# One block for projections and attention, with nine convolution taps moved from ScalarE and DMA to VectorE

## What is computed

```python
proj = h @ w_in                       # q (8 heads of 64), k, v (2 heads), and the two halves of a GLU
kv_ctx = hc @ w_in[:, k and v columns]
q, k = rope(rms_norm(q)), rope(rms_norm(k));  k_ctx = rms_norm(k_ctx)
attn = softmax([sink, q k_ctx, q k within +-128 tokens]) @ [v_ctx, v]
u = depthwise_conv(ga * sigmoid(gb), 31 taps) + conv_b     # 512 channels
u = silu(layer_norm(u))
x = x + g1 * (concat(attn, u) @ w_out)
x = x + g2 * (gated MLP of modulate(rms_norm(x)))          # w_up, width-3 conv, w_down
```

## Time and profile before

| | us |
|---|---|
| median of 3 runs | 1359.11 (1356.21 to 1361.14) |
| the profiled execution | 1354.87 |
| its span in the profile | 1353.0 |
| GLU products | about 60 to 154 |
| projections to q, k, v and the last transposes | about 155 to 255 |
| attention | about 258 to 492 |
| output projection, MLP | the rest, from about 507 |

### The profile page before, as it was taken

The page is one execution under the profiler, slowest core; times in us unless marked ns, Lnnn a source line. Parts: engine busy times, 40 slices in busy tenths (PEclk is TensorE's granted clock), DMA queues, the critical chain, the costliest instruction groups (busy, mean ns, idle before and its releaser), DMA issues. The chain is left out here.

```text
span 1353.0 us, 15984 instructions
## 1 busy us (share of the span) xinstructions
PE 1244.5 (92%) x6181; PEld 1031.7 (76%) x6181; DVE 677.9 (50%) x979; ACT 453.2 (33%) x723; POOL 137.5 (10%) x148
## 2 busy tenths in 40 slices
PE   5899899689869869999999999999999969999997
PEld 1378788589857857877888888888888858887886
DVE  1589955578634544434344444434344444447445
ACT  4542356556535653553222222222222211110110
POOL 2100111254551020000000000000000000004001
PEclk9899989688879979999999999999999989999999
DMA  9222545599994005213111111111111041113112
GB/s 377 66 85 76 121 93 110 125 206 264 256 260 120 1 0 202 79 47 93 47 47 47 47 55 53 47 47 47 47 47 47 16 155 47 47 47 109 47 47 78
DMA packets 86772, 126.77 MB, mean 94 GB/s; under 512 B 6842, under 2 KB 60210, under 8 KB 85700
## 3 DMA queue, kind: packets, MB, share of 16 engines
q1 hardware_dynamic: 75796, 87.65, 19.4%
q0 software_dynamic: 9776, 34.28, 12.8%
q10 hardware_dynamic: 1152, 4.19, 0.8%
HBM read 85.74 MB, written 8.39 MB: 70 GB/s over the span
## 5 line engine op out<-in xcount | busy, mean ns | idle before, releaser
L1331 PE MATMUL ps<-hx,uph 128*128 128x512 f32 x672 | 261.4, 389 | 0.0
L1332 PE MATMUL ps<-hx,uph 128*128 128x512 f32 x672 | 261.4, 389 | 0.0
L1335 PE MATMUL ps<-hx,upl 128*128 128x512 f32 x672 | 206.9, 389 | 0.0
L1133 DVE TENSOR_TENSOR upl<-up_raw,uph 128x1024 fp32r<-128x1024 f32 x44 | 53.8, 1226 | 263.9 <-ACT uph L1130 263.9
L1130 ACT ACTIVATE uph<-up_raw 128x1024 fp32r<-128x1024 f32 x44 | 46.5, 1060 | 339.5 <-PE ps L1335 328.6
L1464 PE MATMUL ps<-dnh,ah 128*128 128x512 f32 x352 | 138.1, 392 | 13.2 <-DVE al L1515 13.2
L1332 PEld LDWEIGHTS ps<-hx,uph 128*128 128x128 f32 x672 | 126.2, 188 | 26.2
L1331 PEld LDWEIGHTS ps<-hx,uph 128*128 128x128 f32 x672 | 126.2, 188 | 26.1
L1335 PEld LDWEIGHTS ps<-hx,upl 128*128 128x128 f32 x672 | 126.2, 188 | 26.1
L1465 PE MATMUL ps<-dnl,ah 128*128 128x512 f32 x352 | 137.5, 391 | 0.0
L1466 PE MATMUL ps<-dnh,al 128*128 128x512 f32 x352 | 137.5, 391 | 0.0
(11 more groups left out here) (235 smaller groups left out, 2159.7 us busy)
## 6 DMA issues: line engine op xcount, KB each, us to landing
up_raw<-in_w_up SPq DMA_DIRECT2D x44, 512.0 KB, 3.8
wm<-in_w_mod SPq DMA_DIRECT2D x32, 512.0 KB, 7.6
sums<-wm POOLq DMA_DIRECT2D x32, 512.0 KB, 8.6
dn_raw<-in_w_down SPq DMA_DIRECT2D x44, 256.0 KB, 2.7
wm<-in_w_mod SPq DMA_DIRECT2D x8, 1024.0 KB, 20.6
conv_y<-u POOLq DMA_DIRECT2D x14, 512.0 KB, 4.5
cacc<-cacc POOLq DMA_DIRECT2D x11, 512.0 KB, 4.5
xs<-in_x ACTq DMA_DIRECT2D x8, 512.0 KB, 14.3
```

The costliest lines, as they stand in the source:

```text
L1133: dve.tensor_tensor(out=upl[:, g], in0=up_raw[:, g], in1=f(uph[:, g]), op=ALU.subtract).then_inc(up_lo, 1)
L1331: pe.matmul(o, uph[:, g, k, :], hx[:, k, 0, c_], start=(k == 0), stop=False)
L1332: pe.matmul(o, uph[:, g, k, :], hx[:, k, 1, c_], start=False, stop=False)
L1335: last = pe.matmul(o, upl[:, g, k, :], hx[:, k, 0, c_], start=False, stop=(k == KT - 1))
```

## The change

1. Blocks s1 and s3 become one: no meeting of the engines between them. Semaphores and buffers are laid out anew; each wait that the block's end had covered is now written out (`drained`, `qkT_out`, `v_out`).
2. The first transposed item comes in tile 3, not in tile 2. Tile m uses the pair of banks of `(m + 2) % 3`.
3. Group 0's scores are issued in tile 8 (behind k = 5 and 6) and tile 9 (behind k = 1 and 2). Its maxima stand on VectorE behind tile 7's low parts (heads 0, 1) and behind tile 8's rotations (heads 2, 3). Its `exps` stand on ScalarE ahead of the reading of tile 8 and of tile 9. Its scores use banks 0 and 1 alone.
4. Tile 8's items follow the loop over tiles; what remains of tile 9 (sums, roots, high and low parts) goes into group 0, its items into group 1 (j = 0 to 2).
5. The summed tile gets 22 products, all in the projections. The other nine taps are VectorE instructions of 1024 columns (`join_taps`), one a group in groups 2 to 6 and two each in groups 7 and 8, behind the join of the two sums in group 1. Products 16 to 21 with an even number go through another buffer.
6. The 153 steps of the other tiles: six instead of twelve behind the last GLU product, 33 instead of 16 in tiles 2 to 7, five a group in groups 1 to 8, none in group 0.
7. GpSimd begins the modulation vectors when the last item has been placed (group 1); SyncE loads their first tiles behind tile 9's matmuls.

```diff
-        TAP_QKV = (0, 0) + (2,) * TT
-        TAP_GRP = 6
+        TAP_GLU = (0, 11, 11, 13, 13, 13, 13, 6)
+        TAP_QKV = (0, 0, 7, 6, 6, 3, 6, 5, 0, 0)
+        TAP_GRP = 5
+        MOVE = 16
-        P_BLOCK = 24
+        P_BLOCK = 22
...
+            return u[:, 0, 0:T] if i % 2 else cacc[:, DVE_TILES[2], :] if i < MOVE else u[:, DVE_TILES[1], 0:T]
...
+            if i == MOVE:
+                act.wait_ge(tap_done, 2 * NCS)
...
+        def join_taps(dve, n):
+            if n == 0:
+                for r in range(2):
+                    dve.wait_ge(sum_in[r], 16 * (P_BLOCK // 2 - 1))
+                ins = dve.tensor_tensor(out=SUM[0], in0=SUM[0], in1=SUM[1], op=ALU.add)
+            else:
+                i = P_BLOCK + n - 1
+                dve.wait_ge(join_done, n)
+                v = SUM[0].rearrange("p (two s) -> p two s", two=2)
+                ins = dve.scalar_tensor_tensor(out=v, in0=by_parity(u_plain[:, i:i + T]), scalar=cols[:, C_CONVW + i * CTL + AT:C_CONVW + i * CTL + AT + 1],
+                                               in1=v, op0=ALU.mult, op1=ALU.add)
+            ins.then_inc(join_done, 1)
+
+        JOINS = TAPS - P_BLOCK + 1
+        JOIN_AT = ((), (3,), (3,), (3,), (3,), (3,), (3,), (1, 3), (1, 3))
...
+            FIRST_SCORES = {(NK - 2, 5): 0, (NK - 2, 6): 1, (NK - 1, 1): 2, (NK - 1, 2): 3}
...
+                sp.wait_ge(qkv_mm, NK)
...
+                pool.wait_ge(qkT_out, len(items))
...
+                def drained(m):
+                    pe.wait_ge(v_out, m + 1)
+                    pe.wait_ge(k_mul, m + 1)
+                    if m >= CT:
+                        pe.wait_ge(q_mul, m - CT + 1)
...
+                    if it == 0:
+                        pe.wait_ge(v_out, NK)
+                        pe.wait_ge(q_mul, TT)
...
-                        if m >= 2 and k in (2, 4, 6) and turned < items_upto[m - 1]:
-                            turn(turned)
+                        if m >= 3 and k in (2, 4, 6) and turned < items_upto[m - 1]:
+                            turn_qk(turned)
                             turned += 1
+                        if (m, k) in FIRST_SCORES:
+                            scores(0, FIRST_SCORES[m, k])
...
+                        if n == 1 and j < 3:
+                            turn_qk(turned)
+                            turned += 1
...
+                    if m >= NK - 2:
+                        for hl in range(2 * (m - NK + 2), 2 * (m - NK + 2) + 2):
+                            exps(0, hl)
+                    read_tile(m)
+                    if m == NK - 1:
+                        break
+                    product(act)
+                    roots(m)
+                    k_high(m)
                     if m >= CT:
+                        q_high(m)
                         product(act)
...
+                        if n == 0 and j == 0:
+                            q_high(NK - 1)
+                        if n == 0 and j == 1:
+                            roots(NK - 1)
+                        if n == 0 and j == 2:
+                            k_high(NK - 1)
+                        if n == 1 and j < 3:
+                            place(placed)
+                            placed += 1
...
-                    elif n == LN - 1:
-                        for r in range(2):
-                            dve.wait_ge(sum_in[r], 16 * len(range(2 + r, TAPS, 2)))
-                        dve.tensor_tensor(out=cacc[:, AT, :], in0=cacc[:, AT, :], in1=conv_y[:], op=ALU.add).then_inc(tap_done, 1)
...
-                            if n < LN:
-                                taps(dve, TAP_GRP if n == LN - 1 and j == 3 else TAP_GRP // 4 + (j < TAP_GRP % 4))
+                            if n == 0 and j == 0:
+                                square_sums(NK - 1)
+                                rope_sums(NK - 1)
+                            elif n == 0 and j == 1:
+                                k_scaled(NK - 1)
+                            elif n == 0 and j == 3:
+                                low_halves(NK - 1)
+                            elif 0 < n < LN:
+                                taps(dve, TAP_GRP // 4 + (j < TAP_GRP % 4))
+                                if j in JOIN_AT[n]:
+                                    join_taps(dve, joined)
+                                    joined += 1
```

More of the change, by code:

```diff
@@ new lines, in values @@
+                def values(n, j):
+                    i, g, kts = head_steps(n)
+                    it = first_item[n] + j
+                    if j == 0 and n:
+                        pe.wait_ge(on_done, n)
+                    if j == 0 and n == 0:
+                        pe.wait_ge(qkT_out, items_upto[NK - 1])
+                    pe.wait_ge(pt_out, it + 1)
+                    for hl in range(GQ):
+                        last = pe.matmul(ps[:, 6, hl * HD:(hl + 1) * HD], pt[:, it % NPT, hl * P:(hl + 1) * P], vraw[:, kts[j], g, :],
+                                         start=(j == 0 and hl == 0), stop=(j == len(kts) - 1), skip_group_check=True)
+                    last.then_inc(pv_mm, 1)
@@ new lines, in turn_outputs, with mean_of @@
+                def turn_outputs(n):
+                    pe.wait_ge(on_done, n + 1)
+                    if n == 0:
+                        pe.wait_ge(qkT_out, len(items))
+                    bank_read(n + 1)
+                    for r in range(2):
+                        last = pe.transpose(ps[:, 7, r * P:(r + 1) * P], on[:, r * P:(r + 1) * P], ident[:])
+                    last.then_inc(oT, 1)
+                def mean_of(buf, hh, signal):
+                    for ct in range(CTL):
+                        last = pe.matmul(ps[:, 7, :], meanw[:], buf(ct)[:, half(hh)], start=(ct == 0), stop=(ct == CTL - 1))
+                    last.then_inc(signal, 1)
@@ L583, in place, with read_tile @@
                     act.activation(dst, src, ACT.Copy).then_inc(qkT_out, 1)
[L585 to L592 removed]
+                def read_tile(m):
+                    b, h0 = slot(m), (0 if m >= CT else NH)
                     act.wait_ge(qkv_mm, m + 1)
@@ new lines, in _ @@
+                placed = 0
+                act.wait_ge(const_done, 7)
+                for m in range(NK):
+                    while m >= 3 and placed < items_upto[m - 1]:
+                        place(placed)
[4 more added lines that the diff above has]
+                    read_tile(m)
+                    if m == NK - 1:
+                        break
+                    product(act)
+                    roots(m)
+                    k_high(m)
@@ L617, in _ @@
+                output_high(NGRP - 1)
+                for i in range(4):
+                    act.wait_ge(row_mm, 4)
+                    act.activation((g1b, g2b)[i // 2][:, half(i % 2)], ps[:, i, :], ACT.Copy).then_inc(row_out, 1)
             @block.vector
```

602 lines of the change are left out of this document (299 added, 303 removed).

## The result

| | before | after |
|---|---|---|
| median | 1360.12 (1356.21 to 1361.59, 4 runs) | 1315.54 (1313.02 to 1318.48, 4 runs) |
| the profiled execution | 1354.87 | 1318.48 |
| its span | 1353.0 | 1316.7 |

The ratio is 0.9677 with a 95% interval of 0.9643 to 0.9712: 44.6 us faster by the medians. The forecast was 1319, 40.0 less than before.

A forecast was written before the change was run, and what follows sets the result against it. TensorE, 92% busy, was taken as the bound, with gains from its idle and 1.2 GHz time. 9.0 - 1.2 + 8.4 + 22.1 + 1.7 = 40.0 off 1354.87 gives 1314.9; the median 4.2 higher, so 1319, range 1312 to 1326.

The forecast's parts named there:

- the seam: Tile 8's end to group 0's outputs: 31.5 us instead of 39.9, saving 8.4 before 1.2 for tile 8's scores.
- groups 1 to 8: Attention, group 0's to group 8's outputs: late products and adds go, 97.8 us against 119.9, saving 22.1.
- first transposes in tile 3: Projections, tile 2: TensorE's 5.83 us hole and 3 us of half clock go; gain taken as 9.0 us.
- scores in tile 8: Two heads' scores, about 0.6 us each, put tile 8's end 1.2 us later.
- group 2: Attention: takes over the burst in which GpSimd's first four multiplies slow VectorE; 14.0 us.
- groups 7 and 8: Attention: VectorE's five steps and two taps make 12.1 us; taken as 12.2 each, 24.4 together.
- behind group 9: Rest of the kernel after group 9: nothing touched, no change counted.
- a seam bound by ScalarE: Rival, chance 0.12: third items wait 4 us more, clock stays down into group 1; seam gives 0, time 1328.
- the moved taps meet GpSimd: Rival, chance 0.20: GpSimd's multiplies lengthen VectorE's taps; groups 1 to 8 save 12.2 instead of 22.1, time 1329.
- The waits were not all small: Rival, chance 0.08: groups at 10.9 us and no stall at third items; 8 us more gained, 1311.
- group 8's wait is gone: Opposing rival, chance 0.05: last adds or late VectorE keep group 8's wait, putting 15 us back; time 1334.
- nothing kept TensorE at 1.2 GHz: Opposing rival (slower), chance 0.03: seam and short waits hold TensorE at 1.2 GHz through group 8; time 1373.

The follow-up runs named there:

- experiment 1: The kernel before with only the first transposed item moved from tile 2 to tile 3; 1352.18 us, ratio 0.9945 against before.
- experiment 10: experiment 5 with all of tile 9's sums, roots, parts and items ahead of group 0's scores; 1320.91 us, ratio 0.9712 against before.
- experiment 5: The changed kernel with group 0's scores, maxima and Exp behind the loop over tiles; 1316.24 us, ratio 0.9667 against before.
- experiment 2: The kernel before without the last seven products of the summed tile and their adds; 1336.41 us, ratio 0.9857 against before.
- experiment 4: The changed kernel without GpSimd's 32 multiplies of w_mod with c, loads and adds kept; 1312.2 us, ratio 0.9637 against before.
- experiment 6: The changed kernel with eight VectorE steps moved from groups 1 to 8: five behind tile 8's low parts, three in group 0; 1313.86 us, ratio 0.9662.
- experiment 3: The changed kernel without the nine moved taps on VectorE, left out of the sum; 1312.11 us, ratio 0.9662 against before.
- experiment 11: The changed kernel with first scores behind the loop, tile 9's roots ahead of group 0's Exp, and VectorE's steps, join and taps spread anew; 1308.62 us, ratio 0.963.

## Why the prediction was right, by its steps

The time was inside the range, 3.5 below the forecast, and the direction and the main causes were as stated. That the sum comes so near is in part luck: the seam saved 2.3 us more than forecast and groups 1 to 8 saved 1.7 less, and the terms were read from an execution of before that was short at the seam and behind group 14, by some 3 us in each place if experiment 1's is the measure. By terms, between the profiled executions:

| step | forecast | measured |
|---|---|---|
| first transposes in tile 3 | 9.0 | 9.8, of which 0.8 ahead of tile 0 (7.6 when made alone, by medians) |
| scores in tile 8 | -1.2 | -1.1 (9.8 less 8.7) |
| tile 8's end to group 0's outputs | 31.5, saving 8.4 | 29.2, saving 10.7 |
| group 1 | 13.0 | 13.8 |
| group 2 | 14.0 | 11.7 |
| groups 3 to 6 | 46.4 | 47.7 |
| groups 7 and 8 | 24.4 | 26.35 |
| group 9 | saving 1.7 | saving 1.6 |
| modulation vectors' last add issued | near 405, price 0 | 394.01, price 0 |
| behind group 9 | untouched, 0 | 5.0 lost, of which 3.5 also in experiment 1 |

**First transposes.** The reasoning holds: no idle time at the item, in after and in experiment 1.

**The seam.** The chain of copies was right to half a microsecond: tile 9's matmuls end at t = 12.7 (13.1 forecast), the waits at the third items are 1.73 and 3.12 us (2.3 and 2.8). What came out better was group 0 behind them, 16.5 us from tile 9's end instead of 18.4. Its first turn begins at t = 17.5 (forecast 18.7), and from there it takes 11.7 us to the outputs (forecast 12.8). In that last part ScalarE is busy for 9.5 us, where the forecast, adding up durations of instructions that in the rows above overlap by about 0.1 us each, had 10.3; the 2.2 us left are near the 2.5 that it had for waits. The load at 229.91 cost nothing: it ends 2.07 us before the sums that its roots need, and the forecast counted nothing for it. The prediction treated the scores in the tiles, the single block and tile 9's remainder as one term, and that hid what the experiments showed: the first is worth under 1 us, the second by itself 0 to 3, the third about 7.5 us at group 0's outputs (263.66 in experiment 10, 256.14 in experiment 5) and 4.7 by the medians. The rival of a seam bound by ScalarE was wrong in its total (it gave 0, and 10.7 were measured) and right about the mechanism, for that part of the change alone.

**Groups 1 to 8.** The largest term, and its cause stands: without the late products (experiment 2) the kernel before has groups of 11.6 us at a clock of 1.00, and the wait of 13.18 us in group 8 is gone in every kernel without them. The size was off by 1.7 us in all, from two errors that partly cancel. Group 2 was put at 14.0 for a burst of four multiplies; it took 11.7. Groups 7 and 8 were put at 12.2 each, by adding up VectorE's work without the multiplies; with two taps and multiplies on each they took 13.2 and 13.1. Groups 3 to 6 are 11.9 instead of 11.6; without the multiplies (experiment 4) groups 3 to 6 took 10.8 each and groups 7 and 8 12.0 and 12.4. The prediction put the wait in group 8 down to full DMA engines; it left out that the last add stands 23.5 us in GpSimd's list first.

**The rival that the moved taps meet GpSimd** was right that the multiplies stretch groups 2 to 8, and wrong about which instructions pay. Taps stayed at 1.27 us but for one of 2.96; the 512-column steps took most of the loss. Its price, 9.9 us, was too high: without any multiply g0 to g8 is 7.7 us shorter, and part of that loss was in the forecast already, since before's groups had it too. The Trainium skill's section named there, taken strictly, would have one instruction wait for the whole of the other; the rows of group 5 show both kinds, a step of 0.74 grown to 1.39 under a multiply, and a tap of 1.28 that kept its time while the multiply that began inside it (314.70) took 1.89 us, longer than the 1.11 and 1.43 of others. The tap of 351.28 does not fit the strict reading: it began 0.45 us before the multiply of 351.73, and yet it was the tap that grew, to 2.96, while the multiply kept 1.43. There the measurement decides.

**The other rivals** fell. The waits were not all small (11.9 us a group, not 10.9); group 8's wait is gone; nothing kept TensorE at 1.2 GHz from group to group: group 1 had a mean clock of 0.81, groups 2 to 6 of 1.00.

**The tail** was the one thing left out. The forecast held everything behind group 9 fixed, and there the profiled execution of after lost 5.0 us at a lower clock. For 3.5 of them the reason lies in before's execution, as experiment 1 shows. The rest stands in group 14, which took 12.7 us in the traces of before and of experiment 1, and 13.8 or more in the other twelve; why is open. Experiments 4 and 6 lost time in group 9 at a lower clock, and experiments 3 and 11 did not. What decides whether such a stretch falls to 1.2 GHz stays open.

## What to carry to other kernels

Look first at work whose result comes by a late transfer: without the late adds and their products g0 to g8 fell by 27 us, the largest single effect here. Ask of such an add both how long it takes under load and how long it stands in its engine's list before it is issued. When scores or any other work of the next stage are pulled forward into a full stage, look at the queue of the engine that must serve both (here ScalarE's Exp beside Sqrt); moving the remainder of the old stage back, beside the new stage, was worth about 7.5 us at that place and 4.7 by the medians, and pulling the new one forward less than 1. When work is moved to an engine that looks half idle, place it where that engine waits (behind the loop and in groups 0 and 1 here), at a single piece per group, and away from a neighbour that slows it; the kernel of experiment 11, which goes by this, is the only one whose times lie clear of the changed kernel's. And before a loss or gain is read from two traces, see where each lies among its kernel's times: one that is 5 us below its median lends its luck to every comparison.

## What the runs showed of the hardware that was not expected

- **Multiplies of GpSimd make a group longer even when VectorE has time left.** With 48.8 us of VectorE's work in five groups (experiment 3) they took 57.8 us, and with 48.5 (experiment 2) 58.2; with 48.4 us and no multiplies (experiment 4), 53.6.
- **A local gain is not always a gain at the end.** Experiments 3, 4 and 6 were 6.5, 7.7 and 6.0 us shorter than after between group 0's and group 8's outputs. At the end the same executions were 8.7, 2.7 and 3.5 us shorter than after's (1318.48), and 3.4, 3.3 and 1.7 by the medians: experiment 3 kept its gain, 4 and 6 lost a good part of it. Group 9 alone, unchanged in work, took 15.5 us at a clock of 0.96 in after, 17.0 at 0.90 in experiment 6 and 18.2 at 0.84 in experiment 4.
- **The same stretch at two levels.** Groups 14 and 15 had the clock at 0.94 and 0.58 in the profiled execution of before, at 0.76 and 0.50 in that of after, with the same instructions. The two largest waits there were 1.84 and 5.02 us before, 1.81 and 4.15 after; group 15 had 0.50 in every trace but before's.
